# Decay exponents of a chunked scan: two 384-column matmuls on a block-diagonal operand and one exponential per step

## The reference

```
a_cs = cumsum(d * a, axis=2)                        # per chunk, per head
seg = a_cs[:, :, :, None] - a_cs[:, :, None, :]     # (l, s)
decay = exp(where(causal, seg, -inf))
cb = einsum('bclgn,bcsgn->bclsg', cc, bc)
y_diag = einsum('bclsgr,bcsgrp->bclgrp', cb[..., None] * decay, xdt)
```

## Time and profile before

| what | value |
|---|---|
| median of 3 runs | 3098.64 us (3098.47 to 3099.03) |
| span of the profiled execution | 3098.5 us |
| PE busy | 3040.6 us, 98% |
| DVE busy | 1498.0 us, 48% |
| ACT busy | 1198.9 us, 39% |
| POOL busy | 1368.7 us, 44% |
| mean granted TensorE clock | 0.993 |
| chain that ended last | PE 78%, issue 10%, POOL 6%, DVE 3% |

### The profile page before, as it was taken

How to read it: one execution, slowest core, us unless ns; L and a number is a source line. 1 busy time by engine, 2 the same in 40 slices (tenths; PEclk the granted TensorE clock), 3 DMA queues, 4 the chain that set the end, 5 groups by cost and what they waited for, 6 DMA issues and landing times.

```text
span 3098.5 us, 41463 instructions
## 1 busy us (share of the span) xinstructions
PE 3040.6 (98%) x14366; PEld 2468.2 (80%) x14366; DVE 1498.0 (48%) x2005; ACT 1198.9 (39%) x2118; POOL 1368.7 (44%) x817
## 2 busy tenths in 40 slices
PE   7999999999999999999999999999999999999997
PEld 6787788888778878888877877888887888888886
DVE  3578715233277751505247774341515787243242
ACT  2355424233344533323344543332334554242233
POOL 1345544444445454444434554444443545444443
PEclk9999999999999999999999999999999999999999
DMA  8322123333332212433333212343334221233333
GB/s 224 102 69 62 55 89 100 120 99 95 110 104 63 67 55 89 134 98 95 95 114 92 69 55 71 93 129 95 96 94 136 63 62 55 87 91 129 98 99 95
DMA packets 374317, 290.31 MB, mean 94 GB/s; under 512 B 9946, under 2 KB 317790, under 8 KB 374126
## 3 DMA queue, kind: packets, MB, share of 16 engines
q1 hardware_dynamic: 374126, 287.87, 31.5%
HBM read 279.45 MB, written 8.39 MB: 93 GB/s over the span
## 4 chain that ended last, share of the span: by engine, by line
PE 78%; issue 10%; POOL 6%; DVE 3%; ACT 1%; DMA 0%; DVEq 0%; POOLq 0%; ACTq 0%; SPq 0%
PE bank L959 43%; PE bank L984 23%; POOL w_lo L357 5%; PE bank L1055 2%; PE bank L1014 2%; PE bank L1060 1%; PE bank L1039 1%; PE bank L1024 1%; PE bank L1008 1%; DVE acc L1219 1%; PE bank L1045 1%; PE bank L1031 1%; DVE pre L1214 1%; PE bank L1033 0%; PE bank L995 0%
## 5 line engine op out<-in xcount | busy, mean ns | idle before, releaser
L357 POOL TENSOR_TENSOR w_lo<-raw,w_hi 128x1024 fp32r<-128x1024 f32 x466 | 1127.3, 2419 | 1476.4 <-ACT w_hi L351 1476.4
L351 ACT ACTIVATE w_hi<-raw 128x1024 fp32r<-128x1024 f32 x466 | 494.0, 1060 | 1613.3 <-PE bank L959 838.3
L959 PE MATMUL bank<-hnT_hi,w_hi 128*128 128x512 f32 x2176 | 863.4, 397 | 6.5 <-POOL w_lo L357 3.9
L959 PE MATMUL bank<-hnT_hi,w_lo 128*128 128x512 f32 x2176 | 851.5, 391 | 0.0
L959 PE MATMUL bank<-hnT_lo,w_hi 128*128 128x512 f32 x2176 | 850.3, 391 | 0.0
L984 PE MATMUL bank<-w_hi,T_hi 128*128 128x512 f32 x1536 | 607.1, 395 | 1.2 <-DVE y L1286 1.2
L984 PE MATMUL bank<-w_hi,T_lo 128*128 128x512 f32 x1536 | 598.8, 390 | 0.0
L984 PE MATMUL bank<-w_lo,T_hi 128*128 128x512 f32 x1536 | 598.2, 389 | 0.0
L959 PEld LDWEIGHTS bank<-hnT_hi,w_hi 128*128 128x128 f32 x2176 | 410.7, 189 | 93.0 <-issue 5.5
L959 PEld LDWEIGHTS bank<-hnT_hi,w_lo 128*128 128x128 f32 x2176 | 409.8, 188 | 86.9
L959 PEld LDWEIGHTS bank<-hnT_lo,w_hi 128*128 128x128 f32 x2176 | 410.8, 189 | 83.0
(11 more groups left out here) (194 smaller groups left out, 2621.1 us busy)
## 6 DMA issues: line engine op xcount, KB each, us to landing
raw<-in_w_ff SPq DMA_DIRECT2D x256, 512.0 KB, 4.0
raw<-in_w_in SPq DMA_DIRECT2D x172, 512.0 KB, 3.8
raw<-in_w_out SPq DMA_DIRECT2D x64, 512.0 KB, 3.8
h<-in_x SPq DMA_DIRECT2D x5, 2048.0 KB, 9.8
F<-in_x SPq DMA_DIRECT2D x4, 2048.0 KB, 9.9
out<-h SPq DMA_DIRECT2D x16, 512.0 KB, 3.5
F<-in_norm_f_w SPq DMA_DIRECT2D x4, 512.0 KB, 5.3
pw<-in_pool_w SPq DMA_DIRECT2D x4, 64.0 KB, 3.0
```

Source lines behind the costliest of these rows:

```text
L351: nc.scalar.activation(w_hi[:, n % 2, :], raw[:, n % RING, :], ACT.Copy).then_inc(w_hi_ready.sem, 1)
L357: nc.gpsimd.tensor_tensor(w_lo[:, n % 2, :], raw[:, n % RING, :], w_hi[:, n % 2, :].bitcast(F32), ALU.subtract).then_inc(w_lo_ready.sem, 1)
L959: mm = nc.tensor.matmul(bank[s][:, :], w[:, k, :], t[:, k, :], start=(k == 0 and j == 0), stop=(k == KT - 1 and j == 2))
```

## The change

The exponent of row s and column l for the six heads of a group is written as one matmul for three heads. The moving operand `seg_l` holds, for each chunk, acsT spread over six 128-column blocks, each multiplied by 0 or 1 so that a row is non-zero only in the block of its head (rows 0 to 55), and under it (rows 64 to 119) the 0/1 pattern alone. The stationary operand `seg_s` holds ones for the rows of the group, and under them minus acsT for the rows of the group. The product is acs[l] - acs[s], so the bias `nacs` falls away, and one exponential reads both banks. `seg_l` is made by DVE in step 0 of each block, four instructions of 56 x 768; `seg_s` is made by ACT for a group at a time, two instructions of 56 x 512, in step 0 and in the c = 0 step of the group before. The order of PE in `slot1` becomes the two L1008 matmuls, then two of contraction 120 and 384 columns. Where it waited at q = 0 for the low part of `acsT`, it waits for `seg_l` when g is 0 and for `seg_s` when c is 0. To make room, `E` and the small buffers of the step sizes lie in the place of `T_lo`, and `acsT` in that of `win_tmp`. The setup has two larger memsets, two small reductions and a copy of 56 x 3072 on DVE.

```diff
-        E = sb("E", [P, HEADS_PER_GROUP, P])
+        E = nc.alloc_sbuf_tensor_at("E", [P, HEADS_PER_GROUP, P], F32, offset=T_lo_at)
...
-        acsT = sb("acsT", [56, TB], F32R)
-        pick = sb("pick", [56, HEADS], F32R)
+        acsT = win_tmp[0:56, 0:TB].bitcast(F32R)
+        head_of = sb("head_of", [56, 8])
+        in_group = sb("in_group", [56, 4])
+        not_group = sb("not_group", [56, 4])
+        seg_l = sb("seg_l", [120, CH, HEADS_PER_GROUP, P], F32R)
+        seg_s = sb("seg_s", [120, 2, TB], F32R)
...
+        seg_l_ready = sig("seg_l_ready", CH)
+        seg_s_ready = sig("seg_s_ready", GROUPS)
...
+                nc.vector.memset(seg_l[:, :, :, :].bitcast(F32), 0.0)
+                nc.vector.memset(seg_s[:, :, :].bitcast(F32), 0.0)
...
+                nc.vector.tensor_copy(
+                    seg_l[64:120, :, :, :],
+                    per_row.unsqueeze(1).unsqueeze(3).to_broadcast([56, CH, HEADS_PER_GROUP, P])
+                    ).then_inc(c_vec, 1)
...
+                def negated_sums(b, g):
+                    nc.scalar.activation(seg_s[0:56, g % 2, :],
+                                         ones[0:56, :].unsqueeze(1).to_broadcast([56, CH, P]),
+                                         ACT.Copy, scale=in_group[:, g:g + 1])
+                    acsT_lo_ready.wait(act, b, 1)
+                    nc.scalar.activation(seg_s[64:120, g % 2, :], acsT[:, :].bitcast(F32), ACT.Copy,
+                                         scale=not_group[:, g:g + 1]
+                                         ).then_inc(seg_s_ready.sem, 1)
...
+                            negated_sums(b, 0)
...
-                        for r in range(HEADS_PER_GROUP):
-                            o = c * HEADS + g * HEADS_PER_GROUP + r
-                            last = nc.scalar.activation(
-                                E[:, r, :], bank[4 + r // 3][:, (r % 3) * P:(r % 3 + 1) * P],
-                                ACT.Exp, bias=nacs[:, o:o + 1])
-                        last.then_inc(exp_ready.sem, 1)
+                        nc.scalar.activation(
+                            E[:, :, :].rearrange("p (j r) l -> p j (r l)", j=2),
+                            decay_ps[:, :, 0:GW], ACT.Exp).then_inc(exp_ready.sem, 1)
+                        if c == 0 and g + 1 < GROUPS:
+                            negated_sums(b, g + 1)
...
                     if q == 0:
-                        acsT_lo_ready.wait(pe, b, 1)
                         down_add.wait(pe, b, 0)
+                    if g == 0:
+                        seg_l_ready.wait(pe, b, c + 1)
+                    if c == 0:
+                        seg_s_ready.wait(pe, b, g + 1)
                     exp_ready.wait(pe, b, q)
...
-                        for r in range(3):
-                            head = g * HEADS_PER_GROUP + 3 * j + r
-                            mm = nc.tensor.matmul(bank[4 + j][:, r * P:(r + 1) * P],
-                                                  pick[:, head:head + 1].to_broadcast([56, P]),
-                                                  acsT[:, cols], start=False, stop=(r == 2))
+                    for j in range(2):
+                        mm = nc.tensor.matmul(
+                            bank[4 + j][:, 0:GW].rearrange("p (r l) -> p r l", l=P),
+                            seg_s[:, g % 2, cols], seg_l[:, c, 3 * j:3 * j + 3, :],
+                            start=False, stop=True)
...
-                            nc.vector.tensor_scalar(nacs[:, :], acs[:, :], -1.0, None, ALU.mult)
...
+                            acsT_lo_ready.wait(dve, b, 1)
+                            for k in range(CH):
+                                nc.vector.tensor_tensor(
+                                    seg_l[0:56, k, :, :],
+                                    acsT[:, k * P:(k + 1) * P].bitcast(F32).unsqueeze(1
+                                        ).to_broadcast([56, HEADS_PER_GROUP, P]),
+                                    head_of[:, 0:HEADS_PER_GROUP].unsqueeze(2).to_broadcast(
+                                        [56, HEADS_PER_GROUP, P]), ALU.mult
+                                    ).then_inc(seg_l_ready.sem, 1)
```

More of the change, by code:

```diff
@@ L163, in build @@
         expa = sb("expa", [P, HEADS])
[L164 to L168, removed]
+        steps_of = E.rearrange("p r l -> p (r l)")
+        v, nv, ev, s_, q_, dA, acs, alast = [steps_of[:, i * NB:(i + 1) * NB] for i in range(8)]
         dtt = sb("dtt", [P, NB])
[L170 to L173, removed]
         ea = sb("ea", [P, NB])
@@ L177, in build @@
         dtw = sb("dtw", [P, NB])
[L178 to L187, removed]
+        small = sb("small", [P, 40])
+        ss2 = small[:, 0:2 * CH].rearrange("p (d t) -> p d t", d=2)
+        ss, rstd, ssf, r2, neg_half, eps = [small[:, (2 + i) * CH:(3 + i) * CH] for i in range(6)]
+        ssy, rsy = small[:, 32:33], small[:, 36:37]
+        bank = [ctx.enter_context(nc.psum_tensor(f"bank{i}", [P, 512], F32)) for i in range(4)]
+        decay_ps = ctx.enter_context(nc.psum_tensor("bank45", [P, 2, 512], F32))
+        bank += [decay_ps[:, 0, :], decay_ps[:, 1, :]]
+        bank += [ctx.enter_context(nc.psum_tensor(f"bank{i}", [P, 512], F32)) for i in (6, 7)]
         W_CONV, W_BIAS, W_NMIX, W_NFFN, W_PSC, W_NSSM = 0, 80, 100, 108, 116, 120
@@ L554, in _ @@
                 steps = Steps(dve, sem("m_step"))
-                nc.vector.memset(acsT[:, :].bitcast(F32), 0.0).then_inc(c_vec, 1)
+                nc.vector.memset(win_tmp[:, :], 0.0).then_inc(c_vec, 1)
                 nc.vector.memset(m_pre, 0.0)
-                steps.link(nc.vector.memset(pick[:, :].bitcast(F32), 0.0))
+                nc.vector.memset(seg_l[:, :, :, :].bitcast(F32), 0.0)
+                nc.vector.memset(seg_s[:, :, :].bitcast(F32), 0.0)
+                steps.link(nc.vector.memset(pick, 0.0))
                 dve.wait_ge(c_pool, 5)
@@ L561, in _ @@
                 nc.vector.tensor_copy(pick[0:24, :], ident[0:24, 0:24])
-                nc.vector.tensor_copy(pick[32:56, :], ident[32:56, 32:56]).then_inc(c_vec, 1)
+                steps.link(nc.vector.tensor_copy(pick[32:56, :], ident[32:56, 32:56]))
+                nc.vector.tensor_reduce(head_of[:, 0:HEADS_PER_GROUP],
+                                        pick.rearrange("p (g r) -> p r g", g=GROUPS),
+                                        mybir.AxisListType.X, ALU.add)
+                steps.link(nc.vector.tensor_reduce(
+                    in_group[:, :], pick.rearrange("p (g r) -> p g r", g=GROUPS),
+                    mybir.AxisListType.X, ALU.add))
+                nc.vector.tensor_scalar(not_group[:, :], in_group[:, :], -1.0, None, ALU.mult)
+                per_row = head_of[:, 0:HEADS_PER_GROUP]
+                nc.vector.tensor_copy(
+                    seg_l[64:120, :, :, :],
+                    per_row.unsqueeze(1).unsqueeze(3).to_broadcast([56, CH, HEADS_PER_GROUP, P])
+                    ).then_inc(c_vec, 1)
                 dve.wait_ge(c_pe, 1)
```

2 lines of the change are left out of this document (added).

## The result

The changed kernel takes 3132.81 us (median of 4 runs, 3127.85 to 3136.46) where the kernel before takes 3098.84 us beside it (3098.47 to 3100.77, 4 runs). The ratio is 1.0106, with a 95% interval of 1.0092 to 1.0121: slower by 34 us. The profiled execution has a span of 3131.7 us, against 3098.5 us before. One of the seven runs of the kernel before that stand beside the last experiment, e12, took 4341.37 us at a granted clock of 0.65, and no comparison here uses it.

A forecast was written before the change was run, and what follows sets the result against it. PE, busy 98%, looked like the bound, but level with DVE in 32 of 64 steps. Savings, w_lo collisions and clock summed to +7.9 us a block, +31.6 over four: 3130 us, range 3062 to 3152.

The forecast's parts named there:

- PE's saving: In `slot1`, exponents take 0.69 us instead of 1.66: 0.96 us saved a step, 61 us over 64 steps.
- bound of 0.64 us: Saving per step in `slot1` if PE still stands still between 128 and 120 rows; about +25 us for the kernel.
- The level steps gain nothing: Steps 1, 2, 4, 5, 6, 8, 9, 10: DVE's chain keeps `y_norm` in place, PE waits 0.96 us longer.
- Step 5: Earlier w_lo gets in behind `y_norm`, ahead of both L1241; the chain of step 6 begins 0.7 to 1.4 us late.
- Steps 6 and 10: Early w_lo comes ahead of `xw` and `y_norm`, PE waits for `y_norm`: +6.4 us a block, 3.2 each.
- Steps 0 and 1: `seg_l` products meet w_lo in step 0, taps run late, w_lo delays `xw` in step 1: +4.7 us a block.
- Steps 3, 7, 11: Steps without taps for n1, `y_norm` 2 us ahead of PE: gain 0.96 us each, -2.9 us a block.
- Steps 12 to 15: Last steps of a block, `y_norm` 2 us ahead of PE: gain 0.96 us each, -3.8 us a block.
- Block end: w_lo comes between DVE's pool sums in steps 14 and 15, the last `y_finish` comes late: +1.9 us a block.
- The clock: Long PE wait in step 1 halves the granted clock: +1.6 us a block; repeats in steps 6 and 10 left to range.
- Setup and exponential: Setup's memsets and copy on DVE cost 0, up to 1 us; one exponential instead of six on ACT: 0.
- chain without collisions: Rival, chance 0.24: `y_norm` holds the level steps but w_lo does no harm; free steps gain 31 us: 3068 us.

The follow-up runs named there:

- e12: The changed kernel with one swap on DVE, `y_low` of the step before ahead of the second taps: 3154.92 us, ratio 1.0177.
- e7: The changed kernel with its two 384-column decay matmuls cut to a contraction over 56 rows: 3147.99 us, one run.
- e6: The kernel before, its six small decay matmuls kept but made 120 rows tall instead of 56: 3153.09 us, ratio 1.0168.
- e3: The changed kernel with the `seg_l` products for chunks 1 to 3 moved from DVE to ACT, one chunk a step: 3125.9 us, ratio 1.0085.
- e5: e4 with w_lo held behind `finish` in group 3 too: 3086.25 us, ratio 0.9956.
- e9: e5 with `y_norm` ahead of `xdt` and `xw` in level steps, and `y_low` ahead of the second taps: 3066.9 us, ratio 0.9896.
- e4: The changed kernel with w_lo held behind `finish` of n1 in groups 0 to 2 and `seg_l` of chunks 1 to 3 on ACT: 3096.56 us, ratio 0.999.
- e11: The kernel before, six small matmuls into two neighbouring banks and one exponential in place of six, bias left out: 3098.91 us, ratio 0.9997.

## Why the prediction was right in sum, and where it was off

Forecast 3130 us, measured 3132.81; forecast 31.6 us more than before, in the profiled executions 33.2. By its own steps:

- *PE's saving.* 0.96 us a step was forecast (its own terms, 1.66 - 0.69, make 0.97). 0.94 to 0.97 us was measured wherever PE alone sets the step. The prediction's bound of 0.64 us, if 120 rows stopped PE as 56 do, is excluded: no stop by issue stands at a step's 120-row loads, and e7 brings the stops back with 56 rows. The rule of the Trainium skill ("TensorEngine Tiling (Array Packing)", Key Properties) that a change of the tiling mode drains the engine agrees with e6 and e7, which put it at 0.17 us for each change between 56 and 128 rows.
- *The gap that the Trainium skill gives ("TensorE: Matmul & The Clock Gate", Back-to-back issue gap).* By estimate it would have made the saving 1.01 us; the measured 0.94 to 0.97 speaks for the spacing in the dense rows instead.
- *The level steps gain nothing.* Right: steps 2, 4, 5, 8 and 9 moved by 0.01 us or less. `y_norm` in step 5 starts 10.38 us into the step, before 10.37.
- *Step 5.* Right to 0.1 us for w_lo (2.55 us, right behind `y_norm`) and L1265 (3.48 us for two instructions). The next w_lo caught the taps (4.49 us), which the prediction had put as an if.
- *Steps 6 and 10.* The failed step is: "in step 6 the w_lo, which is still 0.96 us early, now comes ahead of `xw` and `y_norm`". PE was late before that, in `slot1`, waiting for `y_low`, a wait whose cover I had not asked about. The price, forecast as 3.2 us each, was 2.9 us in step 6, of which 1.4 us is 2.33 less the 0.96 us of the saving, and the rest the clock; in step 10 it was 1.4 us in three blocks and 3.0 in the fourth. Two errors met: the wait was shorter than told, and the half clock, which I had left to the range, came in step 6 of every block. e12 and e6 show that the mechanism as told exists and is one reordering away.
- *Steps 0 and 1.* Forecast +4.7 and +1.6 for the clock, +6.3 in all; measured +6.0 in step 1 and, from the last matmul of unit 7 on, -0.66 in step 0: +5.4. PE waits 0.18 us for `seg_l` (0.1 to 0.2 told), the taps of unit 8 end at 150.88 (150.4 told), and the w_lo ahead of `xw` and the half clock are as told. PE's wait was 4.33 us, where over 6 us was told. e3 shows that the four products' own length is only 2 us of it.
- *Steps 3, 7, 11.* Forecast -2.9, measured -2.86.
- *Steps 12 to 15.* Forecast -3.8, measured -2.75. Step 12 gained nothing. PE waits there for `finish` of the last unit of group 3's share (PE L1055 for L1265, 2.4 us in the four blocks); the step had been 11.35 us before against 11.09 of its neighbours, which is a row I could have read: a step longer than its kind already has a second bound.
- *Block end.* Forecast +1.9, measured about +2.5; the wait is for `yo`, behind a pool sum of 2.87 us, not for `y_finish`, and e5 cut it from 3.05 to 1.20 us. It is not the whole: in the first block 1.5 us had come by unit 0 of the next one, and 1.0 us came behind PE's wait of 4.21 us there, where the granted clock is now 0.50 from 884.61 to 891.44, 6.8 us in place of 3.4. The second half of it:

```profile
888.02:891.44 3.42, 3.42 (x9) 2.65 (x9) 0.46 (x1) 0.00 (x0) 0.00 (x0) 0.50 1.05 379
```

- *The clock.* Where PE stood 4.33 us in step 1 the granted clock fell to 0.50 for 3.4 us in three blocks, as in the earlier trace rows, and for 6.8 us in the fourth. The price of 1.6 us was right: step 10 takes 18.12 us without a half clock and 19.72 us with one.
- *Setup and exponential.* Cost 0 to 1 us forecast for the setup. The last matmul ahead of the first step 0 starts at 142.35 us, before 141.67: 0.68 us later. That is not shown to be the setup's, as the same point lies at 139.95 us in e9 and at 142.53 us in e4, which have the same setup. e11 shows 0 for the exponential.

So terms too high by some 3 us a block (steps 6 and 10 by 2, steps 0 and 1 by 1) met terms too low (12 to 15 by 1.1, the end by 0.6), and the third and fourth block, at 8.2 and 11.6 instead of 6.7 us, added 6 us, nearly all of it half clock. That the sum was nearer than its terms is luck. The rival "chain without collisions", 3068 us, is what e9 reaches at 3066.9, but by another way: three orders had to be changed, and its level steps gain while some others don't.

What stays open: what sets the remaining 0.5 us of step 1 in e4 (17.3 us in place of 16.8), and why one wait of PE is followed by a half clock and another of the same length is not.

## What to carry to other kernels

Where two engines are level, time taken off one moves the requests that it triggers; ask of each such request which instruction it will now meet on an engine that excludes it, and follow one step by hand with the durations of the trace. Then fix the order (hold the transfer or split behind the critical instruction, put what others wait for ahead of what nobody waits for) and only then judge the saving: here the same saving gave +34 us without the orders and -33 us with them (and with three quarters of the `seg_l` products on ACT), and the orders gave nothing without it. A wait that looks like the cause may be the cover of a dearer one, as e12 shows, and a smaller saving may cost more than a larger one (e6, e7).

## What the hardware showed that I had not expected

The granted clock doesn't follow from the length of the last wait alone. Three stretches of the changed kernel, behind the same wait of PE of 2.33 us for T_lo, in step 6 and step 10 of the first block and in step 10 of the fourth (columns: stretch, length, busy PE, PEld, DVE, ACT, POOL, then clock, DMA share and GB/s):

```profile
249.73:253.14 3.41, 3.22 (x12) 2.97 (x13) 3.27 (x8) 1.22 (x2) 0.00 (x0) 0.50 0.52 149
319.05:322.46 3.41, 3.41 (x20) 2.92 (x19) 3.31 (x7) 1.02 (x2) 0.00 (x0) 1.00 0.39 115
2594.61:2598.02 3.41, 3.41 (x13) 2.93 (x12) 3.31 (x7) 1.02 (x2) 0.00 (x0) 0.51 0.44 133
```

The first and the third run at 1.2 GHz, the second at 2.4 GHz, with the same instructions ahead of them. A halved stretch of this length costs 1.6 us (step 10: 19.72 us with it, 18.12 us without). Of the eight waits of 2.33 us in this trace five have a halved stretch behind them, and in e3 all eight. The waits of 3.1 us at the block ends have one in two of four cases in the changed kernel and in all four in e4; those of 1.2 us in e5 have none.

A w_lo that comes while a DVE instruction runs can get in ahead of the next one, though the two stand back to back in DVE's queue: w_lo at 238.50 ahead of the end of `y_norm` at 238.81 (L1265 is recorded from 238.73 and ends 2.2 us late), at 253.75 in e6 ahead of the end of `xw` at 253.92. So it is at all 20 places of the changed kernel where a w_lo comes during a `y_norm` and `finish` follows. It is not without exception: at 152.58 a w_lo came 0.02 us ahead of the recorded start of `xw`, `xw` kept its 0.55 us, and the `finish` behind it took 2.88 us. And the instructions that read one operand from a PSUM bank, `yo` and `y_low`, kept their time in all 15 places of that trace where one of them came next while the w_lo ran. Last, a change of a matmul's height between 128 and 56 rows costs 0.17 us, while 120 and 128 rows mix without a stop.
